# Hybrid decoder step with a top-2 mixture of experts: a new deal of the 32-row blocks to two lanes, x kept in the arena and read back, and separate PSUM banks for the second products

## The reference, cut to what matters

```
x = LN(alpha * x + mix @ w_out)
g_sel = argmax(group logits); top 2 of the 8 experts of that group
y[token] = sum over the 2 experts: gate * ((silu(x @ w1[e]) * (x @ w3[e])) @ w2[e])
x = LN(alpha * x + y)
```

```
layer 0: 1 2 1 1 2 2 2 1  1 2 1 3 2 2 2 2  1 1 2 1 1 2 1 2  1 1 1 1 1 2 1 3   sum 49
layer 1: 1 1 1 1 1 1 1 1  1 1 1 1 1 1 1 2  1 1 1 1 1 1 1 1  4 2 4 9 1 1 5 3   sum 54
```

## Time and profile before

| | us |
|---|---|
| median of 3 runs | 2120.32 (2118.47 to 2121.55) |
| the profiled execution, its own time | 2122.16 |
| its span in the trace | 2120.3 |
| TensorE busy with matmuls | 1533.5 (72% of the span) |
| VectorE / GpSimd / ScalarE busy | 555.6 / 405.1 / 210.8 |
| moved by DMA | 526.21 MB, 248 GB/s on average |
| granted TensorE clock, mean | 0.845 |

### The profile page before, as it was taken

One profiled execution on the slowest core, in us unless ns is written; L12 is line 12 of the kernel. 1 busy time (PEld: TensorE's weight loads), 2 busy tenths in 40 slices (PEclk: granted clock), 3 DMA queues, 4 the chain that ended last, 5 costly groups with the idle time before them and its releaser, 6 DMA issues. The chain is left out here.

```text
span 2120.3 us, 41533 instructions
## 1 busy us (share of the span) xinstructions
PE 1533.5 (72%) x16656; PEld 1038.1 (49%) x16656; DVE 555.6 (26%) x1213; ACT 210.8 (10%) x587; POOL 405.1 (19%) x542
## 2 busy tenths in 40 slices
PE   7998989556657756587399998994546677675670
PEld 6887558523324433344288874682323344343340
DVE  0394342710001000010517834255000001000006
ACT  2111130100000000000021112100000000000000
POOL 2158120111101101011310943011000111110103
PEclk9999689678979988799699977996778889897885
DMA  9311134379998899945341112372999983869863
GB/s 367 131 61 73 57 127 185 135 308 376 390 425 341 360 425 425 389 187 211 144 162 60 61 53 100 104 301 81 425 425 422 385 320 127 368 280 426 320 260 131
DMA packets 75038, 526.21 MB, mean 248 GB/s; under 512 B 14367, under 2 KB 31323, under 8 KB 45915
## 3 DMA queue, kind: packets, MB, share of 16 engines
q1 hardware_dynamic: 64458, 492.21, 57.6%
q0 software_dynamic: 10512, 33.04, 4.3%
HBM read 793.30 MB, written 33.88 MB: 390 GB/s over the span
## 5 line engine op out<-in xcount | busy, mean ns | idle before, releaser
L806 PE MATMUL ps<-arena,xT 128*32 128x256 f32 x7168 | 522.1, 455 | 371.7 <-DMA arena<-in_w 325.7
L806 PEld LDWEIGHTS ps<-arena,xT 128*32 128x32 f32 x7168 | 301.6, 130 | 591.3 <-issue 521.6
L486 PE MATMUL ps<-arena,xT 128*128 128x256 f32 x1920 | 428.6, 384 | 0.9 <-issue 0.9
L486 PEld LDWEIGHTS ps<-arena,xT 128*128 128x128 f32 x1920 | 366.0, 192 | 52.6 <-issue 1.0
L1392 DVE COPY xT<-ps 128x128 f32<-128x128 f32 x112 | 32.7, 292 | 1079.3 <-PE ps L814 1079.3
L822 PE MATMUL ps<-arena,xT 128*32 128x256 f32 x3584 | 216.6, 382 | 31.1 <-DVE xT L1392 22.0
L1569 POOL COPY xT<-xT 128x1 int32 x116 | 23.0, 199 | 1048.5 <-PE ps L795 977.0
L822 PEld LDWEIGHTS ps<-arena,xT 128*32 128x32 f32 x3584 | 108.4, 109 | 111.8 <-issue 33.0
L1571 POOL DMA_INDIRECT xT<-x1d,xT x116 | 114.3, 985 | 58.5 <-POOL xT L1569 56.5
L931 ACT ACTIVATE xT<-ps 128x128 f32<-128x128 f32 x112 | 31.1, 278 | 841.0 <-PE ps L806 841.0
L1015 DVE SCALAR_TENSOR_TENSOR arena<-arena,colpar 128x784 f32<-128x784 f32 x120 | 113.7, 1031 | 0.0
(11 more groups left out here) (231 smaller groups left out, 1244.4 us busy)
## 6 DMA issues: line engine op xcount, KB each, us to landing
arena<-in_w SPq DMA_DIRECT2D x336, 2048.0 KB
arena<-in_w_proj SPq DMA_DIRECT2D x30, 1024.0 KB, 5.2
arena<-in_kv SPq DMA_DIRECT2D x32, 640.0 KB, 5.4
yd<-xT SPq DMA_DIRECT2D x448, 32.0 KB
yd<-arena POOLq DMA_DIRECT2D x17, 512.0 KB, 15.3
rowpar<-in_rowpar SPq DMA_DIRECT2D x2, 2706.0 KB, 15.6
x1d<-x SPq DMA_DIRECT2D x8, 512.0 KB, 7.4
colpar<-in_colpar SPq DMA_DIRECT2D x2, 1252.0 KB, 18.2
```

What stands on the lines that cost most here:

```text
L486: ins = pe.matmul(ps[2 + t][0:n, 0:CW], xT[:, k, 128 * t:128 * t + n], ring[c % 2][:, k, :], start=(k == 0), stop=(k == KT - 1))
L806: ins = pe.matmul(ps[HY + q][r, 0:256], xgT[q][:, k % 2, BLK * (k // 2):BLK * (k // 2 + 1)], w13[q][:, :, k, 128 * j:128 * (j + 1)], start ...
```

## The change

1. **The deal.** The lanes are made from the block counts: `incl` is one running sum over all experts, `limit` compares twice the middle of an expert's blocks with `cut` (0, half, all of the total) plus `force`. Lane 1 starts at expert 16 and wraps round below it. `items` is now worked out on 128 partitions, one for each turn (`which`), and brought into one row by two small matmuls. TMAX goes from 50 to 52, and one more block of `yd` is cleared.
2. **x** lies in the arena, above the expert weights, and is read back from `x1d` after the last stores of a layer. It is not multiplied by alpha; the gates are divided by alpha and the epsilon of the norm by its square.
3. **Routing scratch** `R` lies in `xT`. The strictly triangular mask `before` is replaced by the inclusive `sgu_mask` and a subtraction of 1.
4. **PSUM.** Both lanes turn tokens in `TOKENS = ps[0]` and hidden blocks in `HIDDEN = ps[1]`; first products go to `HB[q] = ps[2+q]`, second products to `YB[q] = ps[4+q]`. The wait for `y_out` moves from `hidden` to `output`.
5. **Parameters.** `colpar` lies in the arena; router weights, convolution state and retention state come by transfers of their own, so that GpSimd's two copies and a fill go. The scale of the retention keys moves into constants.

The core of the diff:

```diff
-TURNS0 = NE // 2
-TMAX = TURNS0 + (2 * NTOK) // BLK
+STEP = 16
+TURNS0 = -(-NE // LANES)
+TMAX = 52
...
+    e, far = np.arange(NE), 1e4
+    cut = np.repeat(2.0 * np.arange(LANES + 1) / LANES, NE)
+    force = np.zeros((LANES + 1, NE))
+    force[0], force[LANES] = -far, far
+    for q in range(1, LANES):
+        force[q, e <= (q - 1) * STEP] = far
+        force[q, e >= q * STEP] = -far
...
+        TOKENS, HIDDEN = ps[0], ps[1]
+        HB = ps[2:2 + LANES]
+        YB = ps[2 + LANES:2 + 2 * LANES]
...
                 for q in range(LANES):
-                    expert_load(0, q, L * NE + FIRST[q])
-                    expert_load(1, q, L * NE + FIRST[q])
-                for q in range(LANES):
-                    expert_load(2, q, L * NE + FIRST[q])
+                    for j in range(3):
+                        expert_load(j, q, L * NE + q * STEP)
...
                     store_rows(q, sp.snap(more + 1))
+                    if q == 1:
+                        for t in range(TILES):
+                            E.done(sp.dma_start(x[0:ROWS[t], t, :], x1d[128 * t:128 * t + ROWS[t], :]), f"x_back{t}", 16)
...
-                def turn_tokens(q, n):
+                def turn_tokens(q, n, drained=None):
+                    if drained is not None:
+                        pe.wait_ge(sem(f"xgT{(q - 1) % LANES}"), drained)
                     pe.wait_ge(sem(f"xg{q}"), n * 16)
...
                 def hidden(q, i):
                     pe.wait_ge(sem(f"xgT{q}"), i + L)
-                    pe.wait_ge(sem(f"y_out{q}"), i)
...
                 def output(q, i):
                     pe.wait_ge(sem(f"hT{q}"), i)
                     pe.wait_ge(sem(f"w2_{q}"), (i + 1) * 16)
+                    pe.wait_ge(sem(f"y_out{q}"), i)
...
-                running(0, NE, 0.0)
-                running(TURNS0 + 1, NE, 0.0)
-                running(1, TURNS0, incl[:, NE - 1:NE])
-                E.link(dve.tensor_tensor(base, incl, nblk, ALU.subtract))
...
+                E.link(dve.tensor_tensor_scan(incl, nblk, nblk, 0.0, ALU.add, ALU.max))
+                total = incl[:, NE - 1:NE]
+                dve.tensor_tensor(start, incl, nblk, ALU.subtract)
+                dve.scalar_tensor_tensor(out=limit, in0=C("cut").rearrange("p (q e) -> p q e", q=Q + 1), scalar=total,
+                                         in1=C("force").rearrange("p (q e) -> p q e", q=Q + 1), op0=ALU.mult, op1=ALU.add)
+                E.link(dve.scalar_tensor_tensor(out=twice, in0=incl, scalar=2.0, in1=nblk, op0=ALU.mult, op1=ALU.subtract))
+                E.link(dve.tensor_tensor(limit, bc(twice.unsqueeze(1), [128, Q + 1, NE]), limit, ALU.is_lt))
...
-                E.link(dve.tensor_tensor(tot, incl[:, NE - 2:NE - 1], incl[:, TURNS0 - 1:TURNS0], ALU.max))
+                E.link(dve.tensor_reduce(tot, size[:, 0:Q], AX, ALU.max))
...
-                E.need("x1_store", 16 * TILES)
-                for t in range(TILES):
-                    ins = dve.tensor_scalar(x[0:ROWS[t], t, :], x[0:ROWS[t], t, :], ALPHA, None, ALU.mult)
-                E.link(ins)
...
                 for t in range(TILES):
                     n = ROWS[t]
+                    E.need(f"x_back{t}", 16)
                     dve.wait_ge(sem(f"y_got{t}"), (L + 1) * 32)
```

More of the change, by code:

```diff
@@ L365, in _ @@
                 out = io["s_ret"][bass.ds(L, 1)].rearrange("a p n -> (a p) n")
-                E.done(sp.dma_start(out, CP("ret_state")), "stores", 16)
+                E.done(sp.dma_start(out, ret_state), "stores", 16)
                 for c in range(NCH + 2, NCH + NOUT):
@@ L782, in _ @@
                 E.need("onehot", 1)
-                place, whose = onehots(R)
+                place, whose = onehots()
                 for k in range(2 * TILES):
@@ L786, in _ @@
                 E.done(ins, "idx_ps")
+                E.need("which", 1)
+                for q in range(LANES):
+                    ins = pe.matmul(YB[1][0:1, q * TMAX:(q + 1) * TMAX], R[:, LANE:LANE + LANES][:, q:q + 1], ident[:, 0:TMAX],
+                                    start=True, stop=True)
+                E.done(ins, "which_ps")
                 E.need("routed", 1)
@@ L1313, in _, with lanes @@
                 E.link(dve.tensor_scalar(nblk, cnti, 1.0, None, ALU.max))
[L1316 to L1324 removed]
+                def lanes(at, rows, n=NE):
+                    ap = R[:, at:at + rows * n]
+                    return ap.rearrange("p (q e) -> p q e", q=rows) if n > 1 else ap
@@ new lines, in _ @@
+                Q = LANES
+                which = lanes(LANE, Q, 1)
+                sums, size, origin, at_turn, over = (lanes(LANE + 4 * k, Q + 1, 1) for k in range(1, 6))
+                limit = lanes(LANE + 30, Q + 1)
+                mass = lanes(LANE + 160, Q + 1)
+                mine = lanes(LANE + 290, Q)
+                shift = lanes(LANE + 390, Q)
+                start, twice, moved = (R[:, LANE + 490 + 32 * k:LANE + 522 + 32 * k] for k in range(3))
+                E.link(dve.tensor_tensor_scan(incl, nblk, nblk, 0.0, ALU.add, ALU.max))
@@ L1376, in _ @@
-                E.done(dve.tensor_tensor(items[0:1, 0, 1, :], lane1, high, ALU.add), "tables")
+                E.link(dve.tensor_scalar(at_turn[:, 0:Q], size[:, 0:Q], -1.0, C("tok")[:, 0:1], ALU.add, ALU.min))
+                E.link(dve.tensor_tensor(at_turn[:, 0:Q], at_turn[:, 0:Q], start[:, 0:NE:STEP], ALU.add))
+                E.link(dve.tensor_tensor(over[:, 0:Q], at_turn[:, 0:Q], sums[:, 1:Q + 1], ALU.is_ge))
+                E.link(dve.tensor_tensor(over[:, 0:Q], over[:, 0:Q], size[:, 0:Q], ALU.mult))
```

232 lines of the change are left out of this document (120 added, 112 removed).

## The result

The changed kernel takes 2185.23 us (median of 4 runs, 2182.6 to 2188.74), against 2120.94 for the kernel before on the same chip: ratio 1.0306, 95% interval 1.0285 to 1.0327, 3.1% slower. The forecast was 2197 us, range 2164 to 2224. The profiled execution has a span of 2186.9 us, 66.6 more than before.

A forecast was written before the change was run, and what follows sets the result against it. Neither DMA engines nor TensorE bound alone: DMA bounds turns loading both lanes, TensorE paces turns without loads. 2120.3 + 97.5 (deal) - 26 (banks) + 0.4 (routing) + 5 (read-back) = 2197.2 us span; median forecast 2197, range 2164 to 2224.

The forecast's parts named there:

- The deal: Expert loops: new lanes give 25 and 37 turns, 62 in all for 56; +97.5 us.
- the price by order: Expert loops: turns priced from rows with the same neighbours; layer 0 529.5 us (-41.3), layer 1 728.2 (+138.8); +97.5.
- The price by kind: Expert loops: turns priced by two, one or no loads (25.8, 22.3, 14.2 us); layer 0 538, layer 1 708; +86.
- the run of double loads: Layer 1's loop, turns 1 to 8: both lanes load every turn, 120.9 us for four, then 4 x 30.8.
- The rival that the bytes rule: Expert loops: same 64 loads set the time, turns without loads hide; total near 2080 us; chance 0.02.
- Banks: Expert loops: own banks end the first product's wait in 20 turns without loads, 1.3 us each; -26 us.
- the 12.6 to 13.4 that I gave as a sign: Expert loops: turns without loads would take 12.6 to 13.4 us; under 10 us would show the forecast wrong.
- the register arithmetic and the jump: Loop overhead that may show once the bank wait goes, so the least gain is half of 32.4, 16 us.
- Read-back: Behind the loops: reading 2.2 MB per layer beside the block outputs' gather; +5 us for both layers, 0 to +12.
- Routing: Before the loops: added operations cost +2.2 to +2.8 us a layer, dropped x scalings give 2.6 back; about +0.4 in two layers.

The follow-up runs named there:

- shared_banks: Changed kernel with both products of a lane in one bank again and the y_out wait back in the first product; 1.0409 of the kernel before.
- step24: Changed kernel with one constant changed, STEP = 24 for 16, so lane 1 starts at expert 24; 2070.56 us, 0.9755 of the kernel before.
- step24_shared_banks: Changed kernel with STEP = 24 and both products of a lane in one bank again; 0.9768 of the kernel before.
- banks_only: Kernel before with only own banks for second products and the y_out wait moved to the second product; 0.9929 of the kernel before.
- no_readback: Changed kernel without reading x back, nothing else changed; 1.0249 of the kernel before.
- early_readback: Changed kernel with the read-back of x issued before the expert loop, right after the tables; 1.0309 of the kernel before.

## Why the prediction was right

**The deal: right in its mechanism, 15 us too dear.** With the banks as before (shared_banks), the loops differ from the kernel before by -48.5 and +130.4, +81.9 us together; the prediction took +97.5. The turn counts were exact. The step that erred is the price by order: its neighbours came from single turns of the other deal. It was 8 us too dear in layer 1 (728 for 719.8), where the 16 empty turns took 13.92 us for my 14.2 (4 us of it), and 7 too dear in layer 0 (529.5 for 522.3). The price by kind comes nearer in the sum (+86), but by luck: it has layer 0 16 us too dear (538) and layer 1 12 too cheap (708), so knowing the run of double loads did help. That the cap at expert 16 is the loss, and not the halving, is shown by step24: the same code with the cap at 24 is faster than before. There layer 1's loop is as long as before the change (589.4), with 29 turns for 28, and the gain is layer 0's, 514.1 us in 25 turns for 570.8 in 28. Own banks are not the reason: with shared banks, step24_shared_banks is 2.3% faster than the kernel before.

**Empty turns are not hidden.** The rival that the bytes rule falls with every STEP: the loads are the same, and layer 1 takes 696, 636 and 589 us with 16, 20 and 24.

**Banks: -26 forecast, -22 measured, for a partly wrong reason.** Every empty turn got cheaper by 1.7 us (changed kernel against shared_banks) to 2.0 us (banks_only against the kernel before), where I had counted 1.3. So they took 12.25 us, under the 12.6 to 13.4 that I gave as a sign. In the second pair that is more than the 1.62 us of idle time in the earlier trace rows. The timeline of an empty turn of the changed kernel shows that the next first product is under way before ScalarE starts to copy:

```profile
1918.15 1.93 PE L846 MATMUL ps<-arena,xT 128*32 128x256 f32 x32 [0.39 <-DVE xT L1433]
...
1919.66 3.40 PEld L828 LDWEIGHTS ps<-arena,xT 128*32 128x32 f32 x64
1919.87 3.66 PE L828 MATMUL ps<-arena,xT 128*32 128x256 f32 x64
1920.22 0.37 ACT L965 COPY xT<-ps 128x256 f32<-128x256 f32 x1 [2.59 <-PE ps L846]
```

It starts 0.2 us before the second product's modelled end (1920.08), with no gap. Twice 0.2 and the 1.62 us of idle time make the 2.0 us. So nothing was left of the wait, and nothing of the register arithmetic and the jump for which I had kept up to half. The Trainium skill's TensorE: Matmul & The Clock Gate (table at its head) has weight loads pulled ahead of running matmuls. Here the trace agrees: the next product's first weight load (PEld L828) starts at 1919.66, 0.4 us before that end. But I counted every empty turn in full, 20 of them, and layer 0 as a whole gained nothing from its four: 0 us in layer 0, 23.6 in layer 1. That -26 and -22 lie so near is in part luck: too small a price and too many turns nearly cancelled. In banks_only, where more empty turns stand between loading ones, 14 of them gave 13 us.

**Read-back: +5 forecast, 2 to 12 measured.** Against no_readback, the traces give 3.8 and 3.4 us more from the first gather to the first use and 1.2 us more in the norm behind it in layer 0, where the second tile waits for its gather too. By the times it is 12, 10 and 2 us in three pairs. The traces of these pairs agree better: the two stretches behind the loops are together 11.0, 7.0 and 6.5 us shorter without the read-back. The half that I took, 5 us, was too little in all three traces. The full 2.2 MB at 426 GB/s, 10.4 us in two layers, fits the first pair (11.0), and is too much for the other two. The Trainium skill's Trainium Kernel Development and Optimization (Key Constraints) says that transfers of the SP and POOL queues share the same 16 engines. The trace agrees, twice: SP's five transfers made POOL's gather behind the loop 3.6 us later, and in early_readback the one before it 3.9.

**Routing: +0.4 forecast, -2.1 measured.** Two stretches stand in the timeline of the changed kernel, layer 1. The rows are the first scan, the operation behind the added ones, `routed`, and the first copy of tokens.

```profile
1399.86 0.23 DVE L1357 TENSOR_TENSOR_SCAN xT<-xT 128x32 f32<-128x32 f32 x1
...
1403.21 0.32 DVE L1377 TENSOR_SCALAR xT<-ps 128x160 int32<-128x160 f32 x1
...
1415.33 0.33 DVE L1407 TENSOR_SCALAR xT<-ps,const 128x104 int32<-128x104 f32 x1 [3.83 <-PE ps L800]
...
1421.70 0.42 DVE L1429 COPY xT<-ps 128x256 f32<-128x256 f32 x1 [3.64 <-PE ps L818]
```

From the first scan to the operation behind the added ones it is 3.35 us where 1.15 stood (408.11 to 409.26 in layer 0), +2.2 us, as forecast. The way from `routed` to lane 1's first SiLU is 16.6 us for 19.5 (layer 0: 17.0 for 20.8). So 2.9 and 3.8 us came back where I allowed 2.6. The first tokens are copied 6.4 and 6.9 us behind `routed` for 9.8 and 10.0 before: they had waited for the scaling of x and now wait for their gather (3.80 us in the row in experiment 6).

**The sum.** By the traces: 81.9 (deal) - 23.0 (banks) + 8.4 (read-back) - 2.1 (routing) = 65.2 for 66.6. The errors of my terms, 15.6 too high, 3.0 and 3.4 too low, 2.5 too high, make 11.7 us of excess, of which the forecast's span shows 10.3. That these nearly add up is partly chance, since the stretches outside the loops differ by up to 4 us from trace to trace. The mechanism of each term was the one forecast; the sizes of the banks' and the read-back's terms erred against that of the deal, and helped it.

## What to carry to other kernels

Count the turns, and then ask of each what it waits for. With the banks as before, balancing by block counts under a cap that the data can push against lost 130 us in one layer while it won 48 in the other, and moving the cap by one constant made the same code the faster kernel. What is won by taking out a wait depends on the turn behind it: in a run of turns that TensorE paces it was kept (23.6 of 26.6 us in layer 1), and beside turns whose transfers fill the DMA engines it was mostly given back (11.3 of 17.3 us in layer 0 of banks_only). A transfer put beside a gather on which work waits made it 3.4 to 3.9 us later here, behind the loop and before it; not moving the 2.2 MB at all was the only variant that gained.

## What the runs showed that was not expected

- A first product of another bank started 0.2 us before the recorded end of the second product ahead of it, so the wait in the record (0.70 and 0.92 us) understated what its removal gave (12.25 us a turn in banks_only for 14.2, about 1 us a block).
- Own banks were worth 22 us with 16 empty turns in layer 1 and 3 us, not clear of noise, with 4: the value of one edit depended on the deal made by another.
- Moving 2.2 MB of read-back from behind the loop to before it changed the total by nothing measurable (1.0309 for 1.0306), though the DMA share over the 47 us behind layer 0's loop (965 to 1012) is only 0.56.
